# Norm weights on ScalarE's queue, all tiles of x on SyncE's in order of need, identity turned meanwhile

## The reference

```python
def rms_norm(x, g):
    xf = x.astype(jnp.float32)
    y = xf * lax.rsqrt(jnp.mean(xf * xf, axis=-1, keepdims=True) + EPS)
    return (y * g.astype(jnp.float32)).astype(x.dtype)

# each layer
h = rms_norm(x, w_norm1)
proj = jnp.einsum('bsd,de->bse', h, w_in)      # short convolution, attention, spatial gating
...
x = x + jnp.einsum('bse,ed->bsd', mix, w_out)
h2 = rms_norm(x, w_norm2)
x = x + jnp.einsum('bsf,fd->bsd', jnp.square(jax.nn.relu(jnp.einsum('bsd,df->bsf', h2, w_ff1))), w_ff2)
# at the end rms_norm(x, w_norm_final); all in float32
```

## Time and profile before

| | |
|---|---|
| median of 3 runs | 2251.72 us (2251.33 to 2251.74) |
| profiled execution | 2251.76 us |
| its span, first to last instruction | 2249.8 us |
| TensorE busy | 2221.7 us, 99% |
| VectorE busy | 1593.1 us, 71% |
| ScalarE busy | 901.6 us, 40% |
| GpSimd busy | 133.7 us, 6% |
| granted TensorE clock, mean | 0.998 |

### The profile page before, as it was taken

One profiled execution on the slowest core, in us unless ns is written; L12 is line 12 of the kernel. 1 busy time (PEld: TensorE's weight loads), 2 busy tenths in 40 slices (PEclk: granted clock), 3 DMA queues, 4 the chain that ended last, 5 costly groups with the idle time before them and its releaser, 6 DMA issues.

```text
span 2249.8 us, 34273 instructions
## 1 busy us (share of the span) xinstructions
PE 2221.7 (99%) x13334; PEld 1978.9 (88%) x13334; DVE 1593.1 (71%) x2603; ACT 901.6 (40%) x1706; POOL 133.7 (6%) x223
## 2 busy tenths in 40 slices
PE   7999999999999999999999999999999999999998
PEld 7988878999999978888899888789999998888886
DVE  5327875788777786776852478668878787867767
ACT  5123432456555523233331234234555555223233
POOL 5011100000000000000130101010000000000002
PEclk9999999999999999999999999999999999999999
DMA  6101012436555776536231100133555558846353
GB/s 182 44 29 43 20 46 78 134 138 220 175 204 176 285 302 240 214 123 224 85 74 38 43 29 20 48 113 118 189 185 193 185 190 331 299 165 233 135 213 112
DMA packets 213617, 330.36 MB, mean 147 GB/s; under 512 B 14524, under 2 KB 98016, under 8 KB 213456
## 3 DMA queue, kind: packets, MB, share of 16 engines
q1 hardware_dynamic: 209888, 321.93, 40.4%
q0 software_dynamic: 2704, 3.10, 0.7%
q10 hardware_dynamic: 864, 3.15, 0.4%
HBM read 212.28 MB, written 115.64 MB: 146 GB/s over the span
## 4 chain that ended last, share of the span: by engine, by line
PE 94%; DVE 3%; ACT 1%; DMA 1%; issue 1%; POOL 0%; SPq 0%; ACTq 0%; DVEq 0%; POOLq 0%
PE ps L2043 29%; PE ps L2044 29%; PE ps L2045 29%; PE ps L2099 1%; PE ps L2240 1%; PE ps L2203 1%; PE ps L2223 1%; DMA ff_ops<-row_op 1%; PE ps L2184 1%; DVE xn L1332 0%; PE ps L2158 0%; PE ps L2180 0%; PE ps L2142 0%; DVE w_lo L1317 0%; DMA x<-in_x_prompt 0%
## 5 line engine op out<-in xcount | busy, mean ns | idle before, releaser
L2043 PE MATMUL ps<-h_all,w_hi 128*128 128x288 f32 (+1 forms) x1408 | 442.6, 314 | 0.8 <-DVE q L1625 0.8
L2044 PE MATMUL ps<-h_all,w_hi 128*128 128x288 f32 (+1 forms) x1408 | 440.0, 312 | 0.0
L2045 PE MATMUL ps<-h_all,w_lo 128*128 128x288 f32 (+1 forms) x1408 | 439.9, 312 | 0.0
L2043 PE MATMUL ps<-w_hi,h_all 128*128 128x512 f32 (+1 forms) x720 | 275.4, 382 | 1.3 <-ACT vn L1083 0.6
L2045 PE MATMUL ps<-w_hi,h_all 128*128 128x512 f32 (+1 forms) x720 | 268.5, 373 | 0.0
L2044 PE MATMUL ps<-w_lo,h_all 128*128 128x512 f32 (+1 forms) x720 | 267.5, 372 | 0.0
L2043 PEld LDWEIGHTS ps<-h_all,w_hi 128*128 128x128 f32 x1408 | 264.7, 188 | 1.7 <-DVE q L1625 1.2
L2044 PEld LDWEIGHTS ps<-h_all,w_hi 128*128 128x128 f32 x1408 | 264.7, 188 | 0.0
L2045 PEld LDWEIGHTS ps<-h_all,w_lo 128*128 128x128 f32 x1408 | 264.6, 188 | 0.0
L2044 PE MATMUL ps<-w_lo,ring_all 128*128 128x512 f32 x544 | 216.5, 398 | 0.0
L2043 PE MATMUL ps<-w_hi,ring_all 128*128 128x512 f32 x544 | 214.2, 394 | 0.0
(11 more groups left out here) (247 smaller groups left out, 4149.7 us busy)
## 6 DMA issues: line engine op xcount, KB each, us to landing
ff_ops<-row_op SPq DMA_DIRECT2D x128, 512.0 KB, 3.3
w_raw<-in_w_ff SPq DMA_DIRECT2D x128, 256.0 KB, 3.7
ring_all<-ff_ops SPq DMA_DIRECT2D x32, 1024.0 KB, 8.0
ring<-ff_ops SPq DMA_DIRECT2D x32, 1024.0 KB, 8.7
ff_raw<-q SPq DMA_DIRECT2D x96, 256.0 KB, 3.5
b_all<-in_w_ff SPq DMA_DIRECT2D x24, 1024.0 KB, 12.3
w_raw<-in_w_in SPq DMA_DIRECT2D x64, 256.0 KB, 3.7
ring<-ff_raw SPq DMA_DIRECT2D x12, 1024.0 KB, 5.7
```

What stands on the lines that cost most here:

```text
L2043: pe.matmul(out, sh, mh, start=first, stop=False)
L2044: pe.matmul(out, sh, ml, start=False, stop=False)
L2045: return pe.matmul(out, sl, mh, start=False, stop=last)
```

## The change

gN is issued by ScalarE as its first instruction. SyncE issues x 0, x 1 and x 2, and x 3 to x 8 between the first four units of weights: unit 0, x 3, unit 1, x 4, x 5, unit 2, x 6, unit 3, x 7, x 8. ScalarE issues no x. TensorE turns the identity onto bank 7 of PSUM 28 times before its loop and four times behind the turn of each of tiles 0 to 3; nobody reads the result.

```diff
             load_x(sp, (0,))
-            sp.dma_start(gN[:], w_norm1[0:1, :].broadcast_to([P, D])).then_inc(*g1_in.tick(None))
             load_x(sp, (1, 2))
...
                     for hk in range(2):
                         cols_unit(2 * cb + hk, 0, in_k, l * KD + 4 * hk, col)
+                        if l == 0 and cb < 2:
+                            load_x(sp, ((3,), (4, 5), (6,), (7, 8))[2 * cb + hk])
...
+            now["l"] = 0
+            act.dma_start(gN[:], w_norm1[0:1, :].broadcast_to([P, D])).then_inc(*g1_in.tick(None))
             act.wait_ge(const_set, 1)
             nc.scalar.activation(es[:], ones[:], ACT.Square).then_inc(tables_in, 1)
-            next_sum(0, 0)
-            load_x(act, range(3, T))
-            for t in range(1, AHEAD):
+            for t in range(AHEAD):
                 next_sum(0, t)
...
+            def keep_turning(count):
+
+                for _ in range(count):
+                    pe.transpose(ps[:, 7, 0:P], ident[:], ident[:])
+
             pe.wait_ge(ident_set, 2)
             pe.wait_ge(const_set, 2)
+            keep_turning(28)
...
                     if t < T:
                         norm_turn(1, t)
+                    if l == 0 and t < 4:
+                        keep_turning(4)
```

## The result

The changed kernel takes 2254.21 us (median of 20 runs, 2252.66 to 2257.05), the kernel before 2251.01 us in the same measurements (20 runs, 2249.91 to 2252.80). The ratio is 1.0015, interval 1.0009 to 1.0021: 3.2 us slower, outside the range of the prediction and on the other side than forecast, though inside 0.2%. The profiled execution is the fastest of its kernel, 2252.66 us with a span of 2250.6 us, and that of before (2251.76 us) is one of the slower of its own. So these two profiles show less than a third of the loss, and the rest had to be looked for in other profiles.

The account below looks back on a forecast made before the run. VectorE's chain up to xn 7 was taken to bound the start, TensorE the rest; 0.23 us from an earlier low 0 plus 0.23 us from the gap gave 0.46 us, a median of 2251.3 us, range 2250.4 to 2253.0.

Parts of the forecast that it names:

- What bounds the kernel: Before 27.98 us VectorE feeds TensorE; a microsecond won on VectorE before xn 7 ends is one of the whole.
- x 0 beside gN: Start, transfers on two queues: x 0 lands at 5.8 us instead of 4.34, sharing with gN.
- the case in which it fits in: Start: x 0 fits into gN's slow transfer, landing at 5.6 us, and x 1 comes 1.23 us earlier, at 6.7.
- gN's full price: Rival, start: x 0 lands with gN at 6.6 us, low 0 0.57 us late; total 2252.1 us, chance 0.15.
- the gap at 14.07: VectorE's 0.23 us wait for ScalarE's h_all copy, from a slow turn of tile 1, goes: 0.23 us won.
- x 1: Start: x 1 lands at 7.2 us instead of by 7.93, so xn 1 comes at 9.37.
- The chain of 2.17 us: Start: time from x landed to xn, 2.17 us, used for tile 0 and tile 1.
- The turned identity: TensorE's start: 28 turns bring the full clock, tile 0's turn taking 1.09 us, not 1.94; covered by 0.7 us at worst.
- Behind 28 us: After the start nearly nothing stops TensorE; 0.01 left on either side for waits of some 5 us that could shift.
- The order of x: Start: x and first weights on SyncE's queue lose nothing; freeing ScalarE of issues is worth nothing.

Follow-up runs that it names:

- no_turns: The changed kernel without any turned identity (44 turns left out): 2252.86 us, ratio 1.0006.
- gn_only: The kernel before with gN issued first by ScalarE and nothing else: 2252.74 us, ratio 1.0008.
- the third profile of the changed kernel: The changed kernel unaltered, profiled alone on another execution, against the kernel before: span 2252.1 us.
- the second profile: The changed kernel unaltered, measured once more against the kernel before: 2255.23 us, ratio 1.0015, span of the profile 2253.8 us.
- gn_back: The changed kernel with gN issued by SyncE again, right behind x 0: 2252.88 us, ratio 1.0004 to the kernel before.
- turns14: The changed kernel with gN on SyncE's queue behind x 0 and only 14 turned identities, all in front: 2250.89 us, ratio 0.9997.
- turns_only: The kernel before with the turned identity alone, 28 in front and four behind each of tiles 0 to 3: 2253.67 us, ratio 1.0009.
- steps88: The kernel before with 88 counting instructions on TensorE ahead of its first turn: 2259.69 us, ratio 1.0044.
- steps256: The kernel before with 256 counting instructions on TensorE, 128 ahead of the first turn, 32 behind each of tiles 0 to 3: 2272.44 us, ratio 1.0097.
- after_page: The changed kernel with 168 counting instructions on TensorE besides, making its code one page longer than before: 2260.98 us, ratio 1.0047.
- gn_back_page: The changed kernel with gN back on SyncE's queue behind x 0 and 168 counting instructions on TensorE: 2261.03 us, ratio 1.0048.

## Why the prediction was wrong

- **What bounds the kernel**: right for the start. VectorE feeds TensorE up to turn 7, and in the runs whose pages stand as before a late start comes out in the time: no_turns is 1.46 us late at 80 us and 1.47 us over before, gn_only 1.83 and 1.83.
- **x 0 beside gN**: wrong. I took 5.8 us, "nearer to the case in which it fits in". Squares 0 started at 6.57, the end of the range that I had worked out as 6.6. The reason that I gave, that one queue alone moves 426 GB/s, says nothing of how long a slow transfer holds the engines. The earlier trace rows held the answer: the DMA share is 0.97 at 213 GB/s and 1.04 at 426, so half the rate fills the engines all the same. The engines were fully taken by gN, so whoever shares them pays. The term was 1.46 us and should have been 2.23. This is the rival "gN's full price", to which I gave 0.15; it had 0.3 us lost (2252.1 less 2251.76), where turn 7 is 0.73 us late, since the gap at 14.07 was taken as gone.
- **x 1**: it was ready at 7.87, by when squares 0 were done, near the 7.93 of the full price. But xn 1 came at 10.84 and not at 10.04, since GpSimd's first step took 0.98 us instead of 0.19 while VectorE worked on xn 0. The chain of 2.17 us that I used for both tiles was 2.97 for the second, and low 0 (12.04) stood behind xn 1.
- **The gap at 14.07**: forecast to go, it stayed (0.30 us) in the first and the third profile of the changed kernel, where turn 1 took 1.97 us, at the half clock, after turn 0 had run at the full one. In the second profile turn 1 took 1.09 us and the gap was gone. I had the full clock for both tiles, and it differs from one execution to the next.
- **The turned identity**: that turns alone bring the clock from 1.2 to 2.4 GHz was right: 1.10 us for tile 0 with them, 1.94 without. The Trainium skill (TensorE: Matmul & The Clock Gate, Part 4) is contradicted for these fp32 turns by gn_back and turns14 as well (turn 0 in 1.09 us). The 28 turns end at 8.04 and cost no time of their own, but with 2.1 us of cover instead of 0.7 only because x 0 was late; in turns_only they end at 7.98 and turn 0 starts at 8.05. What was wrong is that their price was counted in time alone. Their price is 88 instructions of code.
- **Behind 28 us**: the step that failed most. I wrote that nearly nothing stops TensorE there and left 0.01 on either side for "waits of some 5 us in all that could shift". The waits did not shift with the start: the difference stands still within 0.15 us for 350 us. What I put at nothing is that 88 more instructions move every later fetch of TensorE's code. Behind 80 us the changed kernel loses 2.3 us by its median (3.2 us less the 0.87 us of the start), which no term of my sum and no rival held, and kernels whose pages are moved back lose nothing there. Up to 2.3 us of such a loss stand at one fetch, where it is slow; where the rest of the median's loss stands is open.
- **The order of x**: worth nothing, as forecast (0.0 us).

What is shown and what is argued: that the loss behind 80 us comes with the shift by 88 instructions and goes when the pages stand again where they stood is shown by steps88 against steps256, and by the changed kernel and gn_back against the same two with 168 more (after_page, gn_back_page). That the store is late because its share waits on the one engine that fetches code is argued from the times of fetch and wait, which rise together; the trace names no engine for a packet. A rival is not excluded, that a third thing in this burst delays the store and the fetch alike. Why the same kernel's fetch takes 1.08 us once and 2.96 another time, and why its matmuls run slower for some 60 us in some executions, stays open.

## What to carry to other kernels

Work put into an engine's idle time also lengthens its program, and in a long unrolled kernel that moves every later code fetch; before adding some dozens of idle instructions, look in the DMA view at where the fetches of the instruction queue fall against the bursts that a wait hangs on, and compare medians and several profiles, since one may miss the loss (0.75 us of 3.2 here). A slow transfer (here one line read 128 times) can fill the DMA engines: at 213 GB/s their share was 0.97, and x 0 beside it came 2.2 us later. So it belongs behind what is needed first, not beside it: the DMA share, not the GB/s, says whether there is room.

## What was not expected of the hardware

- A code fetch of 16 KB took 0.93 us in a quiet queue and up to 3.06 us among loads with packets of 512 B.
- 88 counting instructions on TensorE ahead of the loop made VectorE 7.46 us late at 80 us, 256 of them (128 ahead of it, 128 in it) 22.44 us. By the start of turn 0 (15.41 us with 88 ahead of it) they take some 0.15 us each, against 0.14 us for a pair of weight load and matmul at full clock (1.10 us for eight).
- In the first profile of the changed kernel the granted clock fell to 0.50 right behind turn 0 (from 11.1 us), where TensorE had stood idle for 2.12 us before it; the four turned identities that follow took 1.01 us and turn 1 took 1.97. In the second profile, idle for 3.41 us at the same place, it did not fall, and turn 1 took 1.09.
- The same matmuls start 0.1767 us apart instead of 0.1733 for some 60 us in some executions, at a granted clock of 1.00.
